# A feed-forward output product by seven block products in place of eight

## The reference

```python
h2 = rms_norm(x, norm_ffn[l])
gu = jnp.einsum('bsd,df->bsf', h2, w_ffn_in[l])            # 1024 -> 2 * 2816
x = x + jnp.einsum('bsf,fd->bsd', jax.nn.silu(gu[..., :D_FF]) * gu[..., D_FF:], w_ffn_out[l])
return rms_norm(x, norm_final)
```

## Time and profile before

| | |
|---|---|
| median of 3 runs | 1576.1 us (1575.4 to 1577.52) |
| profiled execution | 1576.17 us, of it 1574.4 us span |
| PE busy | 1524.8 us (97%), 7853 matmuls |
| DVE busy | 657.7 us (42%) |
| ACT busy | 500.5 us (32%) |
| mean granted clock of PE | 0.993 |
| HBM read, written | 298.29 MB, 4.56 MB |

### The profile page before, as it was taken

One profiled execution on the slowest core, in us unless ns is written; L12 is line 12 of the kernel. 1 busy time (PEld: TensorE's weight loads), 2 busy tenths in 40 slices (PEclk: granted clock), 3 DMA queues, 4 the chain that ended last, 5 costly groups with the idle time before them and its releaser, 6 DMA issues.

```text
span 1574.4 us, 19885 instructions
## 1 busy us (share of the span) xinstructions
PE 1524.8 (97%) x7853; PEld 1067.5 (68%) x7853; DVE 657.7 (42%) x997; ACT 500.5 (32%) x808; POOL 153.0 (10%) x193
## 2 busy tenths in 40 slices
PE   7999999999999999999999999999999999998996
PEld 6788788888888888987777777887434443343333
DVE  6566954334334337675424444476012103004203
ACT  5634644222222225235544443334101010010112
POOL 4000000000000000243101120002000000043101
PEclk9999999999999999999999999999999999999998
DMA  7231233333333324542221112188899999999994
GB/s 219 88 100 55 81 94 99 88 107 86 102 108 83 104 81 132 168 116 81 81 67 55 41 57 78 51 300 329 328 421 421 410 421 421 422 419 422 421 421 191
DMA packets 137818, 305.88 MB, mean 194 GB/s; under 512 B 7584, under 2 KB 97584, under 8 KB 114688
## 3 DMA queue, kind: packets, MB, share of 16 engines
q1 hardware_dynamic: 133616, 294.99, 50.4%
q0 software_dynamic: 3536, 9.12, 2.1%
q10 hardware_dynamic: 576, 0.50, 0.1%
HBM read 298.29 MB, written 4.56 MB: 192 GB/s over the span
## 4 chain that ended last, share of the span: by engine, by line
PE 89%; DMA 4%; DVE 3%; ACT 2%; issue 1%; POOL 0%; POOLq 0%; ACTq 0%; DVEq 0%
PE bank L1288 13%; PE bank L2084 12%; PE bank L2086 12%; PE bank L2085 12%; PE bank L1311 6%; PE bank L2092 4%; PE bank L2094 4%; PE bank L2093 4%; PE bank L2131 3%; PE bank L2224 2%; PE bank L2239 2%; PE bank L2101 2%; PE bank L2102 2%; PE bank L2103 2%; DMA RING<-w_down 2%; DMA RING<-w_gu 2%
## 5 line engine op out<-in xcount | busy, mean ns | idle before, releaser
L2084 PE MATMUL bank<-XH,WH 128*128 128x512 f32 x768 | 303.4, 395 | 2.5 <-DVE XL L1910 2.5
L2086 PE MATMUL bank<-XH,WL 128*128 128x512 f32 x768 | 299.3, 390 | 0.0
L2085 PE MATMUL bank<-XL,WH 128*128 128x512 f32 x768 | 298.9, 389 | 0.0
L1735 DVE TENSOR_TENSOR WL<-RAW,WH 128x2048 fp32r<-128x2048 f32 (+1 forms) x90 | 191.4, 2127 | 128.8 <-ACT WH L1529 128.8
L1289 PE MATMUL bank<-RING,XS 128*64 128x512 f32 x504 | 224.8, 596 | 0.0
L1288 PE MATMUL bank<-RING,XS 128*64 128x512 f32 x488 | 217.9, 595 | 5.3 <-ACT SG L905 3.2
L1529 ACT ACTIVATE WH<-RAW 128x2048 fp32r<-128x2048 f32 (+1 forms) x90 | 160.2, 1780 | 139.4 <-PE bank L2094 114.8
L2084 PEld LDWEIGHTS bank<-XH,WH 128*128 128x128 f32 x768 | 144.2, 188 | 34.4 <-issue 2.9
L2086 PEld LDWEIGHTS bank<-XH,WL 128*128 128x128 f32 x768 | 144.2, 188 | 30.5
L2085 PEld LDWEIGHTS bank<-XL,WH 128*128 128x128 f32 x768 | 144.4, 188 | 29.1 <-issue 0.2
L1288 PEld LDWEIGHTS bank<-RING,XS 128*64 128x64 f32 x488 | 63.7, 137 | 133.7 <-issue 129.2
(11 more groups left out here) (372 smaller groups left out, 2325.5 us busy)
## 6 DMA issues: line engine op xcount, KB each, us to landing
RING<-w_gu SPq DMA_DIRECT2D x120, 1024.0 KB, 15.8
RING<-w_down SPq DMA_DIRECT2D x60, 1024.0 KB, 18.4
RAW<-w_in SPq DMA_DIRECT2D x66, 512.0 KB, 4.7
RAW<-w_ffn_in SPq DMA_DIRECT2D x44, 512.0 KB, 4.6
RAW<-w_ffn_out SPq DMA_DIRECT2D x20, 512.0 KB, 4.6
RAW<-w_out SPq DMA_DIRECT2D x16, 512.0 KB, 4.8
RAW<-w_branch SPq DMA_DIRECT2D x24, 256.0 KB, 2.9
RAW<-w_memkv SPq DMA_DIRECT2D x8, 512.0 KB, 4.4
```

Source lines behind the costliest of these rows:

```text
L1735: V.tensor_tensor(WL[:, u % 2, :n], RAW[:, u % 2, :n], WH[:, u % 2, :n].bitcast(F32), ALU.subtract).then_inc(s["w_lo"], 1)
L2084: T.matmul(bank[:, :st.nt], wh[:, k, c], hi, start=k == 0, stop=False)
L2085: T.matmul(bank[:, :st.nt], wh[:, k, c], lo, start=False, stop=False)
L2086: ins = T.matmul(bank[:, :st.nt], wl[:, k, c], hi, start=False, stop=k == st.K - 1)
```

## The change

For 18 of the 22 tiles the output product is no longer made as eight block products but as seven (the form of Strassen's scheme due to Winograd). The tiles are taken in three groups of six (`GROUPS`). In a group the activations are seen as a matrix of two by two blocks: two halves of 256 tokens, two halves of three tiles; the weights as two by two blocks of three tiles by 512 columns. Each product takes one block or sum of blocks from either side, and the seven results are added into the four blocks of `X`, most of them into more than one.

```diff
+SEVEN = ("a11 b11", "a12 b21", "s1 t1", "s2 t2", "s4 b22", "s3 t3", "a22 t4")
+A_OF = (0, 5, 1, 2, 3, 4, 6)
+LIN_BANKS = (2, 5)
+GROUPS = ((0, 6), (6, 6), (12, 6))
...
-    for f0, nf in ((0, 8), (8, 8), (16, 6)):
-        for f in range(f0, f0 + nf):
-            unit(w_ffn_in[0], P * f, KT, "F", "ffn", f=f - f0)
...
+    for n, (f0, nf) in enumerate(GROUPS):
+        g = Group(n, f0, nf)
...
+        for f in range(nf):
+            unit(w_ffn_in[0], P * (f0 + f), KT, "F", "ffn", f=f, g=g)
+        sevenfold(g)
+    for f in range(4):
+        unit(w_ffn_in[0], P * (18 + f), KT, "F", "ffn", f=f, g=None)
+    for j in range(2):
+        made = unit(w_ffn_out[0], 512 * j, 4, "wide", "accX", src="a", row0=P * 18, later=0, split=2 * j,
+                    lows_later=j == 1)
+    add("ahead", {}, u=len(units))
+    rest(made)
```

**The plan of a group.** `sevenfold` adds a step "sload" (SP loads the four weight blocks: b11 and b12 into the two `RAW` buffers, b22 and b21 into two new buffers `BR`), then seven steps "seven", then a "drain". Weights are split one step ahead, as for units:

```diff
+            elif k == "seven":
+                split_lo(st.u + 1)
+                sevenfold_sums(st)
+                sevenfold_adds(st)
```

**Activations.** Of the first three tiles of a group, DVE writes the product with the gate into `AR`, and high and low parts are made of the first 256 tokens alone. With each of the other three, four sums of 256 columns are made besides, with two waits of DVE on its own results (`link`), and then both high parts and both low parts:

```diff
+                    a11, a21, a12, a22 = AR[:, i, 0:256], AR[:, i, 256:512], fp[:, 0:256], fp[:, 256:512]
+                    link(V.tensor_tensor(AS[:, 0, :], a21, a22, ALU.add))
+                    V.tensor_tensor(AS[:, 3, :], a11, a21, ALU.subtract)
+                    link(V.tensor_tensor(AS[:, 1, :], AS[:, 0, :], a11, ALU.subtract))
+                    V.tensor_tensor(AS[:, 2, :], a12, AS[:, 1, :], ALU.subtract).then_inc(s["sums"], 1)
...
+                          ACT.Copy).then_inc(s["act_hi"], 1)
+                        act.wait_ge(s["sums"], st.end["sums"])
+                        A(AH[:, 1:5, f - g.h, :], AS[:, :, :], ACT.Copy).then_inc(s["act_hi"], 1)
```

**PE.** A product is two token blocks of three tiles, nine matmuls each, with the waits that the scheme needs:

```diff
+            pe.wait_ge(s["w_lo"], st.u + 1)
...
+            wait(pe, "act_lo", st.at, 2 * g.h if i == 0 else 1 if i == 1 else 0)
+            for m in range(2):
+                if st.who:
+                    bank_free(pe, st, st.r0 + m)
+                    bank = LIN[lin_of[st.r0 + m]]
+                else:
+                    before = 24 * g.n + {0: (0, 0), 1: (0, 0), 3: (4, 8), 4: (9, 10), 6: (13, 14)}[i][m]
+                    if before:
+                        pe.wait_ge(s["za"], before)
+                    bank = chain_bank(st, m)
...
+                for k in range(g.h):
+                    hi, lo = AH[:, A_OF[i], k, t], AL[:, A_OF[i], k, t]
+                    fresh = k == 0
+                    T.matmul(bank[:, :], hi, wh[:, k, :], start=fresh, stop=False)
+                    T.matmul(bank[:, :], hi, wl[:, k, :], start=False, stop=False)
+                    ins = T.matmul(bank[:, :], lo, wh[:, k, :], start=False, stop=k == g.h - 1)
```

**Additions into X.** `one_add` adds one bank to 128 tokens by 512 columns of `X`. They stand in `sevenfold_adds`, behind the low part and the sum of the same step: none in the first step, then 4, 4, 4, 2, 4 and 4, and 6 in the drain, which comes ahead of the next unit's bank work. The order of a later step, the fourth:

```diff
+            elif st.s == 3:
+                for m in range(2):
+                    there(p2, m)
+                    one_add(p2, m, m, 0)
+                there(p5, 0)
+                one_add(p5, 0, 2, 1)
+                one_add(p5, 0, 0, 1, "evD")
```

More of the change, by code:

```diff
@@ L77, in __init__ @@
         self.c = self.o = None
+        self.slot = self.need = self.before = self.s = self.g = None
 def number(plan):
@@ L277, in unit @@
         if evac == "ffn":
-            counts.update(act_hi=1, act_lo=1)
+            g = kw["g"]
+            pair = g is not None and kw["f"] >= g.h
+            counts.update(act_hi=1 + pair, act_lo=1 + pair, sums=int(pair), ts=2 * (pair and kw["f"] == 2 * g.h - 1))
         if split:
@@ L286, in unit, with __init__, sevenfold @@
         return st
+    class Group:
+        def __init__(self, n, f0, nf):
+            self.n, self.f0, self.h, self.of = n, f0, nf // 2, []
+    def sevenfold(g):
+        n = len(units)
+        g.first = n
+        g.slot = [0, 0]
+        g.need = [0, 0]
+        g.before = [0, 0]
+        for i, user in enumerate((n + 6, n + 5)):
+            g.slot[i], g.need[i], g.before[i] = take_raw(user)
+        raw_turn[0] = 1 - raw_turn[0]
+        add("sload", {}, a=g)
+        for i in range(7):
+            counts = dict(w_hi=1, w_lo=1, ts=int(i in (1, 4)), za=(0, 4, 4, 3, 1, 4, 2)[i])
+            if i in LIN_BANKS:
+                counts.update(res=2, evD=2)
+            else:
+                counts.update(zr=2)
+            st = add("seven", counts, u=len(units), K=g.h, r0=len(results), who=["dve"] * 2 if i in LIN_BANKS else [])
+            st.cols, st.s, st.g = 512, i, g
+            units.append(st)
+            take_banks(st)
+            g.of.append(st)
+        g.drain = add("drain", dict(za=6), a=g)
     def rest(st, now=None):
@@ L464, in build @@
     tx(XN, XH, XL, KT, TT, scale=V_GFFN, feeds="x")
-    for f0, nf in ((0, 8), (8, 8), (16, 6)):
-        for f in range(f0, f0 + nf):
-            unit(w_ffn_in[0], P * f, KT, "F", "ffn", f=f - f0)
[L468 to L475, removed]
+    group = None
+    for n, (f0, nf) in enumerate(GROUPS):
+        g = Group(n, f0, nf)
+        g.last = group
+        group = g
+        for f in range(nf):
[8 more added lines that the diff above has]
+    rest(made)
     fin = rms(X, XN, D, after=plan[-1], out=True)
@@ L671, in score_bank_free, with finished, raw_weights, blocks @@
                 e.wait_ge(s["p"], q + 1)
+    def finished(e, st):
+        if st.kind == "seven" and not st.who:
+            e.wait_ge(s["zr"], st.end["zr"])
+        else:
+            e.wait_ge(s["res"], st.r0 + len(st.who))
+    def raw_weights(u):
+        st = units[u]
+        n = st.K * st.cols
+        if st.kind == "unit":
+            return RAW[:, st.slot, :n]
+        if st.s in (1, 4):
+            return BR[st.s == 1][:, :n]
+        return RAW[:, st.g.slot[st.s == 5], :n]
+    def blocks(g):
+        n = 512 * g.h
+        return RAW[:, g.slot[0], :n], RAW[:, g.slot[1], :n], BR[0][:, :n], BR[1][:, :n]
+    def chain_bank(st, m):
+        return (SB if st.s in (0, 3) else TR)[m]
     def shaped(st, bank):
@@ new lines, in sevenfold_sums, with one_add @@
+        def sevenfold_sums(st):
+            r0, r1, r2, r3 = blocks(st.g)
+            if st.s == 1:
+                weight_sum(r0, r2, r0)
+            if st.s == 4:
+                dve.wait_ge(br_in[1], 32 * (st.g.n + 1))
+                weight_sum(r0, r0, r3)
+        def one_add(st, m, t, h, done="za"):
+            xs = X[:, t, 512 * h:512 * h + 512]
+            bank = LIN[lin_of[st.r0 + m]] if st.who else chain_bank(st, m)
+            V.tensor_tensor(xs, bank[:, :], xs, ALU.add).then_inc(s[done], 1)
@@ new lines, in sevenfold_drain @@
+        def sevenfold_drain(st):
+            p1, p2, p5, p6, p3, p7, p4 = st.a.of
+            wait(dve, "za", st.at)
+            wait(dve, "evD", st.at)
+            one_add(p6, 0, 0, 1)
+            there(p6, 1)
+            one_add(p6, 1, 3, 0)
+            one_add(p6, 1, 3, 1)
+            one_add(p6, 1, 1, 1)
+            dve.wait_ge(s["za"], st.at["za"] + 2)
+            for m in range(2):
+                there(p4, m)
+                xs = X[:, 2 + m, 0:512]
+                V.tensor_tensor(xs, xs, chain_bank(p4, m)[:, :], ALU.subtract).then_inc(s["za"], 1)
```

189 lines of the change are left out of this document (152 added, 37 removed).

## The result

Over 4 runs the changed kernel takes 1584.96 us (1582.82 to 1586.96), the kernel before 1575.91 in the same rounds: ratio 1.0051, 95% interval 1.0038 to 1.0064. That is 9 us slower, where 1.7 us more than the 1576.1 was forecast; the median lies 0.5 us above the range, and by the ratio (1.0051 of 1576.1, 1584.1) the time would lie just inside it. The profiled execution is the slowest of the four, 1586.96 us, 10.8 more than the 1576.17 of before.

What follows compares the result with a forecast made beforehand. PE was taken to bound the kernel, but the 12.24 us saved turn into waits on DVE and ACT: 1576.17 - 0.06 (groups) + 2.49 (tail) - 0.79 (end) = 1577.8 us, range 1573.5 to 1584.5.

Steps and rivals of the forecast that it cites:

- the walk of the chain: In each group, DVE and ACT steps followed in queue order: stalls 2.95 + 0.17 + 0.94 = 4.06 us against 4.08 saved.
- The second product's low part: DVE's split of the second product's weights ends 6.89 us after T, the group's first product start; PE stalls 2.95 us.
- the fifth's: Stall at a group's fifth product, whose bank needs a DVE addition first: PE 0.17 us late.
- the seventh's: Stall at a group's seventh product, whose bank is free only after one more DVE addition: PE 0.94 us late.
- the rival without overlap: DVE doesn't overlap operations where every addition waits for a bank: groups +2.0 us each, 1583.9 us; chance 0.15.
- the stalls were not hidden: Denies the rival that DVE and ACT keep ahead of PE and only the tail remains, 1565.6 us; chance 0.08.
- the tail's wait: The last four tiles' product waits for all four low parts of its fourth unit: +2.49 us.
- the end's gain: At the stage's end, last additions and the norm get 2.72 us a token block instead of 1.36: -0.79 us.
- the next unit's load: Next group's first weight load, issued after the sixth product's low part, lands at 27.4, ACT takes it at 27.8: no delay.
- the sum: Time of one group of seven products, stalls included: 32.62 us, against 32.64 before.
- the clock falls in the long stalls: Rival: PE's clock halves behind group and tail stalls, 3.1 us lost each: 1590, or 1587 in groups alone; chance 0.11.
- what lies behind moves along with PE: Everything after the feed-forward stage only shifts with PE's time; no term of its own.

Runs made afterwards that it cites:

- e3: Changed kernel with the bank-side parity rule counting one more per group, so ACT and DVE keep their old sides behind the stage; 1583.55 us.
- e1: Changed kernel with twelve filler matmuls ahead of PE's wait for each group's second product and ten ahead of the tail's wait; 1582.16 us.
- e4: Kernel before the change, with its output units waiting for all low parts of their chunk's activations, at all three output products; 1587.21 us.
- b2: Kernel before the change, unchanged, profiled a second time; 1576.48 us.
- e9: e6 with the second product's low part of weights ahead of the last pair's, and its wait for that pair only at its last tile; 1574.13 us.
- e10: e7 with the fourth sum of weight blocks done on 64 of its 1536 columns; 1571.54 us.
- e7: e6 with each DVE addition into X done on 128 of 512 columns, the rest left out; 1571.63 us.
- e6: Changed kernel with the edits of e2 and e3, and the tail's wait for activations' low parts moved to its last tile; 1574.02 us.
- e2: Changed kernel with the second product's weights split by ACT and DVE ahead of the work for the last pair's tiles; 1577.75 us.

## Why the prediction was right in part and wrong in part

**Right: the walk of the chain.** The second product's low part was to end at T+6.89 and ended at T+6.86, each step on the way within 0.03: sums 2.60 (2.61), ACT's copy 3.70 (3.71). Its stall is 2.94 us by the starts (2.95), the fifth's 0.25 (0.17), the seventh's 0.87 (0.94). The three together are 4.06, as forecast. DVE's additions stood 0.60 apart, so the rival without overlap is out; the stalls were not hidden; the tail's wait was 2.45 by the starts (2.49) and the end's gain 0.78 (0.79); the next unit's load, later than forecast (ACT takes it at T+30.1 in place of 27.8; behind the fall it was issued 1.7 later), held that unit by 0.1 us at most. Without falls a group takes 32.84 (e3) to 33.03 us (e1), 0.2 to 0.4 above the sum.

**Wrong: "the clock falls in the long stalls" was a rival at 0.11, and it was the case.** This is the step that failed: the forecast put the price of the clock at nothing. I bounded it by a gap of 4.33 us with a fall and one of 1.67 without, and left 2.3 to 2.8 near the harmless end. Two places are no bound: the trace of before also had a fall behind 1.59 us (under e4), which the prediction passed over. Of the long waits in the stage, four of four in this profile had a fall and nine of twelve in the four profiles, and a granted clock under 1.00 between 330 and 600 us is a sign of being wrong that the prediction itself named. The rival's price was too high (3.1 us from a fall of 6.2; in b2 the same gap has one of 3.4): these last 3.4 us and cost 1.4 to 1.6. Four of them are 6.1 us, the larger part of the miss in the profile. That the loss is not made up, since the fourth product's weights wait for the second, held. The Trainium skill ("TensorE: Matmul & The Clock Gate", section "HAM oscillation — how this bites in real kernels") has waits for DMA between bursts of matmuls, longer ones than these, take the clock down each time anew; the traces agree for nine of the twelve long waits in the stage, not for all.

**Missed: "what lies behind moves along with PE".** It did but for one place: 1.35 us because the number of units changed by an odd number (45 against 34) and a rule on it swapped two engines (e3). No row of the trace could show it; the rule stood in the code.

From the forecast to the profile: 1577.8 + 6.1 (falls) + 1.35 + 0.7 (groups 0.22 above the sum) + 0.4 (0.13 around each group's border) = 1586.4, measured 1586.96. The median is 2 us lower; the three other runs have mean clocks of 0.992 and 0.993 against 0.989. That they had fewer falls fits e3 and e4, but those runs have no trace, so it isn't shown.

That the time lies at the edge of the range and not far outside is luck. The upper bound of 1584.5 was set to take in the rival without overlap, which did not come; the forecast's own part of it ended at 1580.5.

**Where the 12.2 us went, then.** Into waits, as forecast; and, with the clock, into slower matmuls. Behind the first wait stand chains that end almost as late: DVE's queue (e9), the chain of sum, high part and low part for the seventh product, and the next unit's load (e10). Each taken away alone gives a fraction of its size: e7 took some 11 us of DVE's work out of a group and got 0.6.

## What to carry to other kernels

Fewer matmuls are worth little where each carries splits and additions on another engine as long as itself (here 2.9 of 12.2 us at best, in e6); there the order on that engine decides: e2, which moves two calls and removes nothing, gave 7.2 us where 54 matmuls fewer had given none. A wait that is put into a stream of matmuls can have two prices, its length and the lower clock that often came with it here: move the wait behind other matmuls (e6), or keep PE busy through it (e1). And when steps are added to a plan, look for rules that count steps.

## What was not expected of the hardware

- In the feed-forward stage waits of 2.3 to 2.7 us came in nine of twelve cases with 3.4 us at half clock, which began anywhere from 0.36 us ahead of the restart (515.47, with PE idle until 515.83) to 1.3 behind it (317.5 and 316.22). What spares the other three, and why 2.31 us had no fall at 15.11 and 1.59 us had one at 1094.55, stays open.
- A 1536-wide sum on GpSimd took 3.50 us and made a low part of DVE beside it 2.90 long in place of 1.75, and left DVE's additions, which read a bank, at their pace.
